# Gate inputs of the delta rule computed with token tiles as the stationary side

## The reference, cut to what matters

```
u = rms_norm(x, mix_pre_norm[l])
(dq, dk, dv, dz, db, da, sq, sk, sv, gate_a, gate_b) = jnp.split(u @ mix_w_in[l], split_points, axis=-1)
...
beta = sigmoid(beta_logit)                                  # from db, 512 tokens x 4 heads
g = -exp(a_log) * softplus(alpha_logit + dt_bias)           # from da
```

## Time and profile before

| what | value |
|---|---|
| median of 3 executions | 2244.12 us (2244.02 to 2245.47) |
| the profiled execution's own time | 2245.52 us |
| its span, first to last instruction | 2243.7 us |
| mean granted TensorE clock | 0.999 of full |

### The profile page before, as it was taken

How to read it: one execution, slowest core, us unless ns; L and a number is a source line. 1 busy time by engine, 2 the same in 40 slices (tenths; PEclk the granted TensorE clock), 3 DMA queues, 4 the chain that set the end, 5 groups by cost and what they waited for, 6 DMA issues and landing times.

```text
span 2243.7 us, 29247 instructions
## 1 busy us (share of the span) xinstructions
PE 2217.5 (99%) x11476; PEld 1859.5 (83%) x11476; DVE 1006.5 (45%) x1422; ACT 839.7 (37%) x1483; POOL 73.9 (3%) x104
## 2 busy tenths in 40 slices
PE   7999999999999999999999999999999999999998
PEld 7888888788888888888888888887888888888887
DVE  3434324594536443442253433246934355344323
ACT  5323214655533532331252322155554325223211
POOL 0000000010000100000000000010000001000000
PEclk9999999999999999999999999999999999999999
DMA  4232222332123332222232232223311242332232
GB/s 163 94 97 95 98 95 84 130 85 67 57 76 121 107 111 98 98 94 97 82 113 94 93 103 94 99 87 116 92 58 66 79 147 87 102 102 94 94 99 80
DMA packets 71127, 215.84 MB, mean 96 GB/s; under 512 B 18928, under 2 KB 19440, under 8 KB 70256
## 3 DMA queue, kind: packets, MB, share of 16 engines
q1 hardware_dynamic: 69008, 201.82, 27.4%
q0 software_dynamic: 2016, 12.58, 1.5%
HBM read 206.77 MB, written 7.60 MB: 96 GB/s over the span
## 4 chain that ended last, share of the span: by engine, by line
PE 71%; DVE 3%; ACT 1%; DMA 1%; issue 1%; POOL 0%; SPq 0%; DVEq 0%; ACTq 0%
PE ps L510 15%; PE ps L512 15%; PE ps L511 15%; PE ps L558 6%; PE ps L557 6%; PE ps L559 6%; DMA raw<-in_wstream_dram 1%; DVE wlo L1277 1%; PE ps L774 1%; PE ps L719 1%; PE ps L522 0%; DVE tmp L1461 0%; PE ps L795 0%; PE ps L785 0%; ACT whi L897 0%
## 5 line engine op out<-in xcount | busy, mean ns | idle before, releaser
L1277 DVE TENSOR_TENSOR wlo<-raw,whi 128x1024 fp32r<-128x1024 f32 (+1 forms) x376 | 455.9, 1213 | 891.4 <-ACT whi L897 881.6
L510 PE MATMUL ps<-uhi,whi 128*128 128x512 f32 (+1 forms) x2208 | 828.1, 375 | 7.0 <-DVE attnT L1511 3.4
L512 PE MATMUL ps<-uhi,wlo 128*128 128x512 f32 (+1 forms) x2208 | 819.9, 371 | 0.0
L511 PE MATMUL ps<-ulo,whi 128*128 128x512 f32 (+1 forms) x2208 | 819.8, 371 | 0.0
L897 ACT ACTIVATE whi<-raw 128x1024 fp32r<-128x1024 f32 (+1 forms) x372 | 390.4, 1049 | 936.8 <-PE ps L512 547.9
L510 PEld LDWEIGHTS ps<-uhi,whi 128*128 128x128 f32 x2208 | 417.3, 189 | 82.7 <-issue 10.0
L512 PEld LDWEIGHTS ps<-uhi,wlo 128*128 128x128 f32 x2208 | 417.0, 189 | 71.5
L511 PEld LDWEIGHTS ps<-ulo,whi 128*128 128x128 f32 x2208 | 417.4, 189 | 70.0
L557 PE MATMUL ps<-whi,hhi 128*128 128x512 f32 x704 | 274.4, 390 | 0.0
L559 PE MATMUL ps<-whi,hlo 128*128 128x512 f32 x704 | 273.9, 389 | 0.0
L558 PE MATMUL ps<-wlo,hhi 128*128 128x512 f32 x704 | 273.9, 389 | 0.0
(11 more groups left out here) (215 smaller groups left out, 1587.3 us busy)
## 6 DMA issues: line engine op xcount, KB each, us to landing
raw<-in_wstream_dram SPq DMA_DIRECT2D x368, 512.0 KB, 3.4
x_home<-x POOLq DMA_DIRECT2D x4, 1024.0 KB, 4.2
x<-x_home POOLq DMA_DIRECT2D x2, 2048.0 KB, 8.4
gain<-in_gp_dram POOLq DMA_DIRECT2D x6, 512.0 KB, 6.4
x<-in_x_dram SPq DMA_DIRECT2D x4, 512.0 KB, 8.5
raw<-in_wstream_dram SPq DMA_DIRECT2D x8, 256.0 KB, 3.6
out_dram<-x SPq DMA_DIRECT2D x8, 256.0 KB, 2.0
rcs<-in_rope_dram POOLq DMA_DIRECT2D x2, 512.0 KB, 3.9
```

The lines of the kernel that those rows point to most:

```text
L510: pe.matmul(o, lh, bhi, start=first, stop=False)
L511: pe.matmul(o, lh, blo, start=False, stop=False)
L512: return pe.matmul(o, ll, bhi, start=False, stop=last)
L1277: dve.tensor_tensor(wlo[:, s, 0:cols], raw[:, s % RAWS, 0:cols], whi[:, s, 0:cols].bitcast(f32), ALU.subtract) \
```

## The change

Step `ba` now takes 128 tokens of `uhi` or `ulo` as the stationary side and streams the 16 columns of `bab` over it, for each of 4 token tiles, 8 channel tiles and the two parts. The output has tokens on the partitions at once: 16 columns for each token tile, 64 in all, in bank 5. VectorE copies the 8 columns of the high part to `ba` and then adds the 8 columns of the low part from PSUM. Step `bat` is gone. `gprep` waits for `ba`.

```
-    s[4] = [("bat",), ("gprep",), ("silu", 0), ("conv", 1)]
+    s[4] = [("gprep",), ("silu", 0), ("conv", 1)]
...
-    if k in ("ba", "bat", "gsum", "vwin", "sc", "qtr"):
+    if k in ("ba", "gsum", "vwin", "sc", "qtr"):
...
+        ba_part = sem("ba_part", 1)
...
-                        for i in range(KT):
-                            both = bab[:, 16 * i:16 * i + 16]
-                            pe.matmul(bank(5, 0, SEQ, 0, 16), both, uhi[:, i, :], start=i == 0, stop=False)
-                            last = pe.matmul(bank(5, 0, SEQ, 0, 16), both, ulo[:, i, :], start=False, stop=i == KT - 1)
-                        done(last, 5)
-                    elif k == "bat":
-                        use(L, step, 5)
                         for t in range(TT):
-                            last = pe.matmul(bank(5, t * 8, 8), tmp[0:16, 2, t * P:(t + 1) * P], con[0:16, K_I8:K_I8 + 8], start=True, stop=True)
+                            for i in range(KT):
+                                both, tok = bab[:, 16 * i:16 * i + 16], slice(t * P, t * P + P)
+                                pe.matmul(bank(5, 16 * t, 16), uhi[:, i, tok], both, start=i == 0, stop=False)
+                                last = pe.matmul(bank(5, 16 * t, 16), ulo[:, i, tok], both, start=False, stop=i == KT - 1)
                         done(last, 5)
...
                     if k == "ba":
                         ready(step, 5)
-                        dve.tensor_copy(tmp[0:16, 2, :], bank(5, 0, SEQ, 0, 16)).then_inc(misc_out[5].h, 1)
-                    elif k == "bat":
-                        ready(step, 5)
-                        dve.tensor_copy(ba[:, :], bank(5, 0, 32)).then_inc(misc_out[5].h, 1)
+                        parts = bank(5, 0, 64).rearrange("p (t o c) -> p t o c", o=2, c=8)
+                        dve.tensor_copy(ba[:, :].rearrange("p (t c) -> p t c", c=8), parts[:, :, 0, :]).then_inc(ba_part.h, 1)
+                        dve.wait_ge(ba_part.h, ba_part.at(L, 1))
+                        dve.tensor_tensor(ba[:, :].rearrange("p (t c) -> p t c", c=8), ba[:, :].rearrange("p (t c) -> p t c", c=8),
+                                          parts[:, :, 1, :], ALU.add).then_inc(misc_out[5].h, 1)
                     elif k == "gprep":
-                        got(("bat",), 5)
+                        got(("ba",), 5)
```

## The result

| kernel | median us | lowest to highest | runs |
|---|---|---|---|
| before | 2244.07 | 2243.67 to 2245.47 | 4 |
| changed | 2259.74 | 2256.16 to 2263.66 | 4 |

The measured ratio is 1.0063, with a 95% interval of 1.0051 to 1.0075: the changed kernel is slower. The two medians lie 15.7 us apart, where the forecast was 4.5 and the range ended at 2254.5. The changed kernel scatters over 7.5 us in these four executions, the one before over 1.8 (over 4.8 in 20 later ones). The profiled execution took 2256.16 us (span 2254.3) and is the shortest of the four, so its trace shows the mildest form of what follows.

The account below looks back on a forecast made before the run. TensorE, busy nearly the whole span, was taken as the bound. Per layer 7.14 us added less 4.90 removed gave +2.24, two layers +4.5, on the median 2244.1: 2248.6 us, range 2247.0 to 2254.5; other engines costed at nothing.

Parts of the forecast that it names:

- The plain price: TensorE at the gate product: 4.90 us removed, 64 loads at 0.1115 (7.14 us) added, net +2.24 us a layer.
- slower pace of f32r: Rival, chance 0.17: the 64 new matmuls run 0.120 us apart, +5.6 us in all, 2249.7 us.
- two passes: Rival, chance 0.05: each new f32r matmul makes two passes, 128 x 0.112 us, +9.4 us a layer, 2262.9 us.
- loads that hide better: Rival, chance 0.04: loads run wholly under their predecessors, pace 0.081 us, +0.3 us a layer, 2244.7 us.
- VectorE, ScalarE and the stall: Work beside TensorE's path, and TensorE's 1.72 us wait for VectorE at 509.42: all costed at nothing.
- Not slower: the stall shortens: Rival, chance 0.08: VectorE's head start nearly removes TensorE's 1.72 us wait in each layer; +1.1 us, 2245.2 us.
- The cover of the gate chain: VectorE's `g` near 423.3, `gsum` on TensorE at 427.0: 3.7 us to spare, so costed at nothing.
- no other effect: Main forecast, chance 0.50: pace 0.109 to 0.112 us and nothing else, +4.2 to +4.6 us, 2248.6 us.
- clock falls (0.16): Rival, chance 0.16: the 7 us of 16-column matmuls end at the low clock level; +9.7 us, 2253.8 us.
- a next chunk at 0.43 a matmul: Sign that the forecast is wrong: the chunk after the product runs at 0.43 us a matmul, the low clock level.
- the loss of the start phase: First group at the kernel's start: 28 matmuls at 0.21 instead of 0.12 us, 2.6 us lost, taken as price per layer.
- the 1.00 in the earlier trace: Granted clock column at the kernel's start, read as 1.00 although the matmul pace, 0.21 us, showed the 1.2 GHz level.

Follow-up runs that it names:

- cols128: The changed kernel with each of the 64 loads streaming 128 columns instead of 16, the added ones unused; 2249.72 us, ratio 1.0016 to the kernel before.
- before_plus64: The kernel before with the 64 new matmuls put ahead of its own gate product as pure extra work in both layers; 2268.44 us, ratio 1.0096.
- spread: The changed kernel with its 64 matmuls cut into four token tiles, one after chunk 3 and three inside chunk 4; 2251.58 us, ratio 1.0025 to the kernel before.
- rowgroups: The kernel before, narrow product kept, its four transposes spread over four row groups and four banks; 2245.01 us, ratio 0.9995.

## Why the prediction was wrong

**The plain price was right.** Removed 4.90, added 64 x 0.1115 = 7.14, net +2.24 a layer: cols128, the same stretch without the fall, has +2.25 (and its median is 3.4 us above the kernel before, where two layers make 4.5, with an interval that holds both). One record for each matmul and 0.11 between starts held, with 16, 32, 64 and 128 columns alike, as long as the level was high. So the rivals "slower pace of f32r", "two passes" and "loads that hide better" fell. The Trainium skill ("TensorE: Matmul & The Clock Gate", "Back-to-back issue gap") gives 81 ns for a pair of load and matmul at 128 moving columns. No run here reaches it: the pairs of cols128 stand at 0.11.

**VectorE, ScalarE and the stall were right.** I costed them at nothing, and before_plus64 shows the loss without any of their changes. "Not slower: the stall shortens" fell: it was 1.72 us again in layer 1, and in layer 0 slow matmuls filled it. The cover of the gate chain was real but not large: in `spread`, where the last tile comes only after 18 of chunk 4's 24 matmuls, `gsum` waits 0.3 us for `g`.

**The step that failed is the clock, which the forecast's sum put at nothing ("no other effect") and left to the rival "clock falls (0.16)".** The prediction's own sign for it, a next chunk at 0.43 a matmul, is what the trace shows, and the low level cost 4.8 us a layer on the mean of four layers, more than twice the 2.25 of the loads. First its chance. The Trainium skill ("TensorE: Matmul & The Clock Gate", Part 1) says that activity releases the throttle and idleness brings the low level back. This trace shows the low level coming back with no idle time at all: TensorE is busy for 5.06 of the 5.06 us before the fall and 3.63 of the 3.63 behind it. The trace of before had 0.6 us of full loads with 16 columns at most, so it couldn't speak about 7 us of them. But it had a longer stretch of narrow work that the prediction didn't weigh: the solve's 64x64 matmuls with 32 columns stand together for 3.8 us.

```profile
535.39 1.12 PE L719 MATMUL ps<-Z,Pm 64*64 64x32 f32 x32
...
539.23 0.71 PE L774 MATMUL ps<-skz,sq 128*128 128x128 f32 x4
```

In the trace of before the level holds there; the short falls of `spread` (541.6 us) and `cols128` (540.0) come at the end of this same stretch. I then let "TensorE's queue has no gap in it" count against the fall. Every run with the unbroken 16-column stretch fell in both layers of its trace, with TensorE's busy share at 100%. The busy record of an engine whose time goes into loads says nothing on how much it streams, and that is the side that cols128 shows to matter.

**Second its price.** I took 2.6 us a layer, the loss of the start phase, as if the level fell at the end of the stretch and slowed only what came behind. In the five traces with the level falling in the stretch it fell after 21 to 50 of the 64 matmuls, the remaining small ones slowed from 0.111 to 0.213, and in the changed kernel the loss was 3.2 to 6.5 a layer. With the four layers of the two profiles of the changed kernel (3.2, 4.8, 6.5, 4.8) the mean is 4.8, and 2 x (2.25 + 4.8) = 14.1 us against the 15.7 measured, and 11.9 in the second measurement. So even the rival's 2253.8 was too low, and the range that it bounded missed.

**What stays open.** Why the level fell with 64 columns a load and held with 128, and whether it is the columns or something that goes with them, isn't settled by these runs. Nor is how often the level falls outside the change: the trace of before has no such fall, but its 35 later executions have mean granted clocks from 0.997 to 1.000 and times from 2244.56 to 2249.33 us, so some of them probably lost time in the same way. And the prediction took the 1.00 in the earlier trace rows for a reading of the granted clock; it is a stretch without a record, as before_plus64 shows.

## What to carry to other kernels

Turning a product so that the large side becomes the stationary one trades few wide streams for many full loads; price it at the pace that the nearest rows give, here 0.11 us for each 128-column load, before anything else. That price alone, 7.14 us against 4.90, spoke against this change. And if such matmuls would stand together for some microseconds, put them between wide ones: the same 64 cost 2.7 us a layer in four pieces, 5.6 in two and 5.5 to 8.7 in one.

## What the runs showed that I had not expected

- TensorE's clock fell to half in the middle of an unbroken run of instructions (window 411.70 to 415.33 at 0.50, busy throughout).
- The low level slows the loading of the stationary side as well: 0.213 from one load and its matmul to the next in place of 0.111, records of 333 ns in place of 192.
- Streaming 112 useless columns with each load made the kernel faster (ratio 1.0016 against 1.0050 in the same comparison).
- The same kind of fall happens in places that no edit touched, in these traces mostly at or behind the solve's small matmuls. In the profiled execution of rowgroups seven matmuls of the chunk behind the solve's 64x64 work run slow, about 1.6 us lost, more than the edit had saved:

```profile
1647.80 0.72 PE L778 MATMUL ps<-skz,sq 128*128 128x128 f32 x4
1648.26 0.68 PE L512 MATMUL ps<-uhi,whi 128*128 128x512 f32 x1
1648.74 0.63 PE L513 MATMUL ps<-ulo,whi 128*128 128x512 f32 x1
```
